# Moving the window mask, and the order in which ScalarE copies, empties banks and rounds weights

## The reference

```python
def neighbourhood_attention(q, k, v, rpb):          # odd layer, 8 heads of 64
    c0 = jnp.clip(col - kc // 2, 0, GRID_W - kc)
    in_win = (col[None, :] >= c0[:, None]) & (col[None, :] < c0[:, None] + kc)
    bias = table[:, dr_idx[:, None, None], dc_idx[None, :, :]]
    bias = jnp.where(in_win[None, None], bias, -jnp.inf)
    sc = einsum('bhqd,bhkd->bhqk', qr, kb) + bias
    return einsum('bhqk,bhkd->bhqd', softmax(sc, axis=-1), vb)

def memory_cross_attention(h, m, w_q, w_kv, qk_gain, w_o):
    q = rms_norm(heads(h @ w_q, CA_HEADS), qk_gain[0]) * (CA_HEAD_DIM ** -0.5)
    k, v = jnp.split(m @ w_kv, 2, axis=-1)          # the "memory units" of the kernel
    ...

def hybrid_mixer(h, positions, w_in, ...):
    o_fox, o_dsa, o_sb = (three attentions)
    g = sigmoid(gates)                              # (tokens, 3, 1024)
    merged = g[0] * (o_fox @ w_fox_out) + g[1] * (o_dsa @ w_dsa_out) + g[2] * (o_sb @ w_sb_out)
    return merged @ w_out
```

## Time and profile before

| | us |
|---|---|
| median of three runs | 2357.86 |
| lowest and highest of them | 2357.22, 2362.98 |
| the profiled execution, first to last instruction | 2356.1 |
| TensorE busy in it (matmul) | 2238.9 |
| VectorE busy | 1505.8 |
| ScalarE busy | 1111.5 |
| GpSimd busy | 339.3 |
| granted TensorE clock, mean | 0.973 |

### The profile page before, as it was taken

The page is one execution under the profiler, slowest core; times in us unless marked ns, Lnnn a source line. Parts: engine busy times, 40 slices in busy tenths (PEclk is TensorE's granted clock), DMA queues, the critical chain, the costliest instruction groups (busy, mean ns, idle before and its releaser), DMA issues.

```text
span 2356.1 us, 40460 instructions
## 1 busy us (share of the span) xinstructions
PE 2238.9 (95%) x17488; PEld 2137.2 (91%) x17488; DVE 1505.8 (64%) x2188; ACT 1111.5 (47%) x1341; POOL 339.3 (14%) x292
## 2 busy tenths in 40 slices
PE   8988999998789999999999999999999999998998
PEld 7877899997679999999998789999999998898998
DVE  5665687833458788566766657566666556656665
ACT  5445544535455445334646455335334455555333
POOL 2760000045000000000535210000000015310000
PEclk9989999998899999999999999999999999999999
DMA  8642355543224555555653444555555643353552
GB/s 267 195 157 90 118 182 185 179 145 108 72 90 167 193 179 186 172 192 176 163 167 114 129 163 147 175 188 170 179 197 179 168 148 117 117 185 129 182 193 90
DMA packets 314660, 374.21 MB, mean 159 GB/s; under 512 B 23127, under 2 KB 280931, under 8 KB 313331
## 3 DMA queue, kind: packets, MB, share of 16 engines
q1 hardware_dynamic: 309555, 354.88, 46.2%
q0 software_dynamic: 3424, 11.50, 1.7%
q10 hardware_dynamic: 1504, 5.26, 0.6%
HBM read 362.43 MB, written 9.18 MB: 158 GB/s over the span
## 4 chain that ended last, share of the span: by engine, by line
PE 83%; DVE 9%; ACT 5%; issue 2%; DMA 0%; ACTq 0%; SPq 0%; DVEq 0%
PE banks L868 23%; PE banks L869 22%; PE banks L871 22%; PE banks L901 3%; PE banks L902 3%; DVE wlo L1766 3%; PE banks L905 2%; ACT whi L1338 2%; PE banks L1116 2%; PE banks L1154 1%; PE banks L1140 1%; PE banks L1036 1%; DVE wk L2301 1%; PE banks L1023 1%; PE banks L878 1%
## 5 line engine op out<-in xcount | busy, mean ns | idle before, releaser
L868 PE MATMUL banks<-x_hi,wlo 128*128 128x256 f32 (+1 forms) x4344 | 1104.3, 287 | 22.5 <-DVE wlo L1766 6.9
L869 PE MATMUL banks<-x_lo,whi 128*128 128x256 f32 (+1 forms) x4344 | 1094.8, 285 | 0.0
L1338 ACT ACTIVATE whi<-raw 128x2048 fp32r<-128x2048 f32 (+1 forms) x340 | 637.7, 1878 | 618.0 <-PE banks L871 570.3
L868 PEld LDWEIGHTS banks<-x_hi,wlo 128*128 128x128 f32 (+1 forms) x4344 | 840.4, 193 | 42.6 <-issue 19.6
L869 PEld LDWEIGHTS banks<-x_lo,whi 128*128 128x128 f32 (+1 forms) x4344 | 841.1, 194 | 0.0
L1766 DVE TENSOR_TENSOR wlo<-raw,whi 128x2048 fp32r<-128x2048 f32 (+2 forms) x292 | 656.9, 2260 | 167.5 <-ACT whi L1338 167.4
L871 PE MATMUL banks<-x_hi,whi 128*128 128x256 f32 x4344 | 688.8, 284 | 0.0
L871 PEld LDWEIGHTS banks<-x_hi,whi 128*128 128x128 f32 x4344 | 596.9, 193 | 3.2
L836 POOL TENSOR_TENSOR wlo<-raw,whi 128x512 fp32r<-128x512 f32 x184 | 238.2, 1332 | 1168.0 <-ACT whi L1338 1168.0
L901 PE MATMUL banks<-x_hi,wlo 128*128 128x256 f32 (+1 forms) x632 | 169.6, 302 | 23.2 <-DVE xT L1795 7.4
L902 PE MATMUL banks<-x_lo,whi 128*128 128x256 f32 (+1 forms) x632 | 162.6, 291 | 0.0
(11 more groups left out here) (252 smaller groups left out, 1977.7 us busy)
## 6 DMA issues: line engine op xcount, KB each, us to landing
raw<-in_ffn_w_gu SPq DMA_DIRECT2D x88, 1024.0 KB, 5.1
raw<-in_ffn_w_down SPq DMA_DIRECT2D x66, 1024.0 KB, 5.2
raw<-in_ffn_w_up SPq DMA_DIRECT2D x44, 1024.0 KB, 5.1
raw<-in_w_in SPq DMA_DIRECT2D x42, 1024.0 KB, 5.3
raw<-in_ca_w_kv SPq DMA_DIRECT2D x16, 1024.0 KB, 5.2
raw<-in_od_w_in SPq DMA_DIRECT2D x12, 1024.0 KB, 5.1
raw<-in_ev_w_in SPq DMA_DIRECT2D x10, 1024.0 KB, 9.1
raw<-in_w_in SPq DMA_DIRECT2D x20, 512.0 KB, 5.1
```

Source lines behind the costliest of these rows:

```text
L868: eng.matmul(out, a[1], b[0], start=first and i == 0, stop=False, skip_group_check=True)
L869: eng.matmul(out, a[0], b[1], start=False, stop=False, skip_group_check=True)
L1338: eng.activation(whi[s % SETS][:, 0:ch["n"]], raw[i % SLOTS][:, 0:ch["n"]], ACT.Copy).then_inc(S["weights_hi"], 1)
```

## The change

Four edits. The mask is added at the end of VectorE's part of the norms' stage that precedes the neighbourhood attention (`window=True`), ahead of the barrier. In ScalarE's `fill`, which is shared by all stages that have one, `evac_upto` now comes before `split_upto`. In `in_units` on ScalarE, at i = number of units the last back(i-1) comes before the fill of that slot, which is otherwise unchanged for all earlier i.

```diff
@@ odd_mixer
-            heads_norm([...], HD, "rows_odd", fill={"pre": (N[1], N[0]), 0: (N[2], N[1]), 1: (N[3], N[2])})
+            heads_norm([...], HD, "rows_odd", fill={"pre": (N[1], N[0]), 0: (N[2], N[1]), 1: (N[3], N[2])}, window=True)
@@ ScalarE
             def fill(st, slot):
 
                 if slot in st["fill"]:
+                    evac_upto(st["fill"][slot][1])
                     split_upto(reach(st, slot))
-                    evac_upto(st["fill"][slot][1])
@@ ScalarE, in_units
                     if sticks(i - 1):
                         stick_probs(i - 1)
+                    if i >= len(units) > i - 1:
+                        back(i - 1)
                     fill(st, i)
-                    if 0 <= i - 1 < len(units):
+                    if 0 <= i - 1 < len(units) - 1:
                         back(i - 1)
@@ VectorE, end of heads
+                if st.get("window"):
+                    eng.wait_ge(S["bias_loaded"], 16 * BIAS_DMAS)
+                    n = na_bias.rearrange("p h t k -> p (h t) k")
+                    step(eng.tensor_tensor(n, n, C("na_window").unsqueeze(1).to_broadcast([P, 16, SEQ]), ALU.add))
@@ VectorE, in_units
                 if units[0].get("tables"):
-                    eng.wait_ge(S["bias_loaded"], 16 * BIAS_DMAS)
-                    n = na_bias.rearrange("p h t k -> p (h t) k")
-                    step(eng.tensor_tensor(n, n, C("na_window").unsqueeze(1).to_broadcast([P, 16, SEQ]), ALU.add))
                     hold()
```

More of the change, by code:

```diff
@@ L538, in odd_mixer @@
             na, df = prow["od_na_qk_gain"], prow["od_diff_qk_gain"]
-            heads_norm([(t, 2, na + t // 4) for t in (0, 2, 4, 6)], HD, "rows_odd", fill={"pre": (N[1], N[0]), 0: (N[2], N[1]), 1: (N[3], N[2])})
+            heads_norm([(t, 2, na + t // 4) for t in (0, 2, 4, 6)], HD, "rows_odd", fill={"pre": (N[1], N[0]), 0: (N[2], N[1]), 1: (N[3], N[2])}, window=True)
             attention("softmax", [small_heads(o, 0, 4, (h, h + 1), 0, 0, bias=lambda h: na_bias[:, h], tables=True) for h in range(0, 8, 2)],
```

## The result

The changed kernel has a median of 2381.7 us over six runs (2379.3 to 2386.4). Six runs of the kernel before give 2360.8 us (2357.2 to 2363.2). The ratio is 1.009, 95% interval 1.0078 to 1.0103: slower by 18 to 24 us, 21 in the medians. The forecast was +14.1 us on 2357.86, 2372.0 us, with a range up to 2376.5. The sign and the place were right; the size was not, and the time lies above the range.

A forecast was written before the change was run, and what follows sets the result against it. TensorE, busy 2238.9 of 2356.1 us, was taken as the bound, so only its gaps count. Terms 0 - 2.9 + 3.8 + 13.2 = +14.1 us on 2357.86 gave 2372.0 us, range 2365.5 to 2376.5.

The forecast's parts named there:

- The mask: End of the norms' stage: the moved mask fills VectorE's idle time and delays nobody, 0 us.
- Emptying first: ScalarE's fills: -3.4 us in the differential attention, +0.5 in the mLSTM stage, -2.9 us in all.
- The last copy in the odd layer: End of the neighbourhood attention: K[0] waits for later rounded weights from GpSimd, +3.8 us.
- The last copy in the hybrid layers: Slot 9: late rounding holds VectorE, so M[2] waits; 4.7 us plus 1.9 for the clock per layer, 13.2 both.
- the clock: Behind the gap at M[2]: half clock for 3.8 us of work, 1.9 us lost per hybrid layer.
- the loss twice: Upper bound per hybrid layer, with the clock loss counted twice: 8.5 us.
- The rival with more passed on: Hybrid layers: the slow stretch holds twice per layer, +17.9 us in all, 2375.8 us; chance 0.09.
- The gap without its clock: Hybrid layers: TensorE waits as computed but slow clock costs nothing, +10.3 us in all, 2368.2 us; chance 0.15.
- VectorE does not stop at the subtraction: Hybrid slot 9: output(7) or M[0]'s emptying isn't behind the subtraction, no hybrid cost, 2358.8 us; chance 0.10.
- Prompt copying pays: Neighbourhood attention's earlier last copy gains 1.9 us, hybrid late rounding free; 4.8 us faster in all, 2353.1 us; chance 0.04.
- the prediction's own sign: Whole kernel: the prediction is wrong if other stages move by more than 1 us.

The follow-up runs named there:

- e1_mask: Kernel before with only the mask moved ahead of the barrier; 0.9989, 2360.3 us.
- e10: Changed kernel with 20 added useless 128-row matmuls behind each gap, ahead of M[2], run again beside the changed kernel; 1.0063.
- e11: Changed kernel with 20 added useless 64-row matmuls behind each gap, ahead of M[2]; 1.0137, 2394.1 us.
- e6: Changed kernel with 44 added useless 128-row matmuls between turn(8) and the wait ahead of M[2], both hybrid mixers; 1.0043, 2372.9 us.
- e5: Changed kernel with slot 9 set to (M[2], M[2]), so VectorE empties M[0] and M[1] before the late rounding; 1.0009, 2364.6 us.
- e3_copy_first_odd: Kernel before with only the neighbourhood attention's last copy put ahead of its fill; 1.0023, 2367.4 us.
- e2_empty_first: Kernel before with only ScalarE's emptying of banks put ahead of the rounding; 0.9998, 2362.7 us.
- e4: Kernel before with only the two hybrid attentions' last copy put ahead of its fill; 1.0121, 2392.1 us.
- e7: Changed kernel with 20 added useless 128-row matmuls behind each gap, ahead of M[2], first run; 1.0078, 2381.6 us.

## Why the prediction was wrong

The mask: right. It was put at 0 and took none of TensorE's time. The Trainium skill (GPSIMD Engine Reference, § Specifications) names contention between GpSimd and a VectorE instruction with two SBUF inputs. These traces agree, but the size was not as assumed: the mask grew from 4.43 to 4.94 us (5.12 in e1_mask), and the GpSimd subtraction beside it from 1.27 to 5.47 us. The prediction reckoned with 1 us of overlap and looked only at the mask; GpSimd's work was stretched over the whole of it. The zero held because VectorE had 2.44 us to spare and GpSimd 1.3; a kernel with less would have paid.

Emptying first: right. -3.4 us was forecast for the differential attention, -3.1 and -3.7 were traced; the next late thing was K[3]'s bank, as said. In the mLSTM stage TensorE's wait went from 0.46 to 0.94 us, +0.5.

The last copy in the odd layer: right. +3.8 forecast, +3.5 and +4.6 traced, released by GpSimd.

The last copy in the hybrid layers: mechanism right, one term wrong by its size. The gap was forecast at 5.57 us and is 5.54, its own cost 4.7 and is 4.68. The step that failed is the clock: "the granted clock is 0.50 (1.2 of 2.4 GHz) for the next 3.8 us of work" was read off the mLSTM stage and carried to the merges. It was 1.9 us per layer and measures 6.8 and 5.7 us (58.4 - 51.6 and 57.2 - 51.5). The work behind the gap in the mLSTM stage is of another kind: nine of its ten matmuls in those 3.8 us have 128 rows. In the merges a third of the row blocks have 64, and over them the clock took 17.1 to 20.5 us to rise. That the rows are the reason is supported by e10 and e11, but only for the added matmuls. The bound given for it, "the loss twice", was 3.8 us, still too low. That is 4.9 + 3.8 = 8.7 us too little for both layers. The rival with more passed on (0.09) had the right sign and a wrong mechanism: the cost is one low stretch that lasts 17 us and more, and the second one, where there is one, costs 0.7 us. The gap without its clock (0.15) is refuted by e6, which shows what the clock took. That VectorE does not stop at the subtraction (0.10) is refuted by its 9.45 us of idle time there and by e5. Prompt copying pays (0.04) is refuted too: in the hybrid layers the copy starts right behind turn(8) in both kernels and so gains nothing. The rule quoted for it, in the Trainium skill (PSUM — Partial Sum Buffer, § Summary: rules for kernel authors), gives the small size of PSUM as its reason; it promises no time for a copy put first, and "would give this time" was the prediction's own reading.

With these sizes the hybrid layers cost 13.2 + 8.7 = 21.9 us and the whole 14.1 + 8.7 = 22.8. The merge stretches of the two profiled executions differ by 23.3 (58.4 + 57.2 - 46.9 - 45.4); the 1.4 us between 21.9 and 23.3 lie in the second layer, and e6 does not get them back either. The profiles differ by 28.5. Ahead of the first hybrid mixer the changed one is 4.5 us late: 2.6 of that arise in the first 90 us of the program, and their cause stays open, and 3.2 in one stretch near 1180, where the low clock lasts 10.2 us in place of 3.4. That stretch has 3.4, 6.8 or 10.2 us of low clock in all fourteen profiles, whatever the edit (before and e3_copy_first_odd 3.4, e6_busy_in_gap 10.2), so I take it for noise of the single execution, although by the prediction's own sign (no other stage moves by more than 1 us) it would count against it.

A second, smaller error goes the other way. The profiled execution of before was a lucky one: it has no low clock over M[0] to M[3] in either layer, and little behind them. In the four profiled executions whose hybrid mixers are as before, the sum of the two merge stretches is 92.3 (before), 101.8 (e1_mask), 101.0 (e2_empty_first) and 92.3 us (e3_copy_first_odd). The low clock comes into the merges now and then with no longer gap than the 0.99 us that TensorE waits ahead of M[0] in every run, e.g. in e2_empty_first over M[0] and M[1]:

```profile
1314.40:1325.50 11.10, 11.10 (x49) 8.65 (x50) 3.06 (x5) 1.96 (x2) 0.21 (x1) 0.60 0.58 192
```

Against the mean of the four, 96.9, the changed kernel's 115.7 is 18.8 us more; with +3.5, -3.1 and +0.5 elsewhere that is 19.7, beside 20.9 measured in the medians (18 to 24). It may also be why the base moved: three runs of before gave 2357.9, six gave 2360.8, and e5, without the gap at M[2], had 17.1 us of low clock in both layers in its profile, beginning 12 us behind M[2]'s start, and was still within 3 us of before.

The chances were right in kind (slower by over 0.3% had 0.86). The range was too narrow because the clock's cost was bounded by twice one row from another kind of work.

## What to carry to other kernels

Before an engine is made to wait earlier, list what stands behind its next instructions on the engines that wait for it: here a copy that could not come earlier pushed back a rounding nobody needed yet, and that held VectorE in front of a bank that TensorE needed at once. The cheapest repair was to empty the banks ahead of the wait, one number.

The gap on TensorE cost its length and then the clock, here more for the clock (5.7 to 6.8 us) than for the length (4.7). The second part must be read from a stretch with the same kind of matmuls behind it, rows per matmul included. Where the gap was not avoided, useless 128-row matmuls inside it gave back 11 us.

A wait of 0 on the engine you watch is not the whole price of a move: look at the instructions beside it on the other engines too, as at GpSimd's here.

## What the runs showed of the hardware

The granted clock has its two levels, 0.50 and 1.00 (1.2 and 2.4 GHz), in all these rows; a window with a figure between them has part of each. The gap of 5.5 us at M[2] stood in twelve layers (the changed kernel twice, e4, e7, e10, e11). The clock fell in eleven of them, and in the twelfth it was low already. It also fell in merges with no gap over 1 us. It rose again after 6.8 us in all where 20 matmuls of 128 rows came first (four of four, at most 1.3 us behind the last of them), after 17.1 to 20.5 us where the merges came directly (six of six: the changed kernel twice and e4), and after 23.9 us where 20 matmuls of 64 rows came first; in e11's second layer, 22.6 us behind the first of those 20. I had not expected a TensorE that is busy all the time to stay at half the clock for that long. Work with 64-row matmuls is not the only such case. In the stretch near 1180 the clock falls, in the profiles of before and of the changed kernel, with no gap right ahead, over or just behind matmuls of 128 rows that read 14 columns each; the window of the changed kernel (columns as above):

```profile
1174.20:1184.40 10.20, 10.20 (x50) 10.20 (x50) 10.10 (x13) 6.74 (x10) 9.55 (x7) 0.50 0.65 206
```

Why it falls there in one execution for 3.4 us and in another for 10.2, no run shows.

The Trainium skill (TensorE: Matmul & The Clock Gate, § Part 1: The HAM clock gate) says that the gate is set by how busy TensorE has been; in the windows of e11 TensorE is busy, as the profile counts it, for all of 10.1 us and the clock is 0.50. There that page and the measurement differ, and the measurement decides.

VectorE's mask and GpSimd's subtractions behave like two that take turns. Alone the mask takes 4.43 us and a subtraction 1.27. In all ten kernels with the moved mask it takes 0.35 to 1.15 us longer, each time 0.14 or 0.15 us less than what was left of the subtraction running at its start; and in nine of them the next subtraction takes 5.46 to 5.48 us and ends 1.1 to 1.2 us behind the mask, as if its work had begun there. In the tenth, e7, the running one was the last, and it took 1.26 us.
